# Transposed block inverse taken from a transpose of the updated one, in place of a third product per level

## The reference

```python
m = jnp.where(strict, jnp.einsum('bhnid,bhnjd->bhnij', kb, k) * decay, 0.0)
a_mat = m + jnp.eye(C, dtype=m.dtype)
rhs = jnp.concatenate([v * beta[..., None], kb * jnp.exp(gc)[..., None]], axis=-1)
uw = lax.linalg.triangular_solve(a_mat, rhs, left_side=True, lower=True, unit_diagonal=True)
```

## Time and profile before

| | us |
|---|---|
| median of three runs | 1123.85 |
| profiled execution, device time | 1124.4 |
| its span (first to last instruction) | 1122.6 |
| PE busy | 1055.5 (94%) |
| DVE busy | 707.6 (63%) |
| ACT busy | 582.1 (52%) |
| POOL busy | 116.7 (10%) |

### The profile page before, as it was taken

The page is one execution under the profiler, slowest core; times in us unless marked ns, Lnnn a source line. Parts: engine busy times, 40 slices in busy tenths (PEclk is TensorE's granted clock), DMA queues, the critical chain, the costliest instruction groups (busy, mean ns, idle before and its releaser), DMA issues. The chain is left out here.

```text
span 1122.6 us, 17149 instructions
## 1 busy us (share of the span) xinstructions
PE 1055.5 (94%) x7154; PEld 945.9 (84%) x7154; DVE 707.6 (63%) x1027; ACT 582.1 (52%) x869; POOL 116.7 (10%) x111
## 2 busy tenths in 40 slices
PE   2699988899999999999999999999999989999997
PEld 2599978888899788877988889988988969988996
DVE  5679775586685467577655656455446786555554
ACT  3355545643465455545567655444446886444443
POOL 1100016562040001122000010000000200000000
PEclk9999999999899999999999999999999999999999
DMA  9766433532368733223633336555553435555550
GB/s 325 231 187 187 149 115 112 188 114 82 84 187 255 260 122 113 75 76 113 205 133 113 112 123 216 188 187 184 189 183 121 150 126 185 193 186 188 181 181 37
DMA packets 120428, 178.42 MB, mean 159 GB/s; under 512 B 5188, under 2 KB 80098, under 8 KB 120352
## 3 DMA queue, kind: packets, MB, share of 16 engines
q1 hardware_dynamic: 118816, 172.40, 47.3%
q0 software_dynamic: 1120, 2.97, 0.9%
q10 hardware_dynamic: 416, 1.97, 0.5%
HBM read 176.27 MB, written 1.05 MB: 158 GB/s over the span
## 5 line engine op out<-in xcount | busy, mean ns | idle before, releaser
L1334 DVE TENSOR_TENSOR sb_w_lo<-sb_raw,sb_w_hi 128x2048 fp32r<-128x2048 f32 (+2 forms) x141 | 319.6, 2267 | 217.9 <-ACT sb_w_hi L705 217.6
L705 ACT ACTIVATE sb_w_hi<-sb_raw 128x2048 fp32r<-128x2048 f32 (+2 forms) x141 | 265.9, 1889 | 141.6 <-PE G L2135 112.2
L2133 PE MATMUL X<-sb_hT_hi,sb_w_hi 128*128 128x256 f32 x960 | 273.2, 285 | 4.0 <-DVE sb_hT_lo L1664 2.1
L2134 PE MATMUL X<-sb_hT_lo,sb_w_hi 128*128 128x256 f32 x960 | 271.1, 282 | 0.0
L2135 PE MATMUL X<-sb_hT_hi,sb_w_lo 128*128 128x256 f32 x960 | 271.0, 282 | 0.0
L2133 PEld LDWEIGHTS X<-sb_hT_hi,sb_w_hi 128*128 128x128 f32 x960 | 183.1, 191 | 6.5 <-issue 3.0
L2134 PEld LDWEIGHTS X<-sb_hT_lo,sb_w_hi 128*128 128x128 f32 x960 | 183.2, 191 | 0.6
L2135 PEld LDWEIGHTS X<-sb_hT_hi,sb_w_lo 128*128 128x128 f32 x960 | 183.2, 191 | 0.0
L2133 PE MATMUL G<-sb_w_hi,sb_uT_hi 128*128 128x512 f32 x304 | 121.5, 400 | 4.8 <-DVE sb_uT_lo L2073 4.8
L2135 PE MATMUL G<-sb_w_hi,sb_uT_lo 128*128 128x512 f32 x304 | 120.8, 397 | 0.0
L2134 PE MATMUL G<-sb_w_lo,sb_uT_hi 128*128 128x512 f32 x304 | 120.5, 397 | 0.0
(11 more groups left out here) (442 smaller groups left out, 1793.7 us busy)
## 6 DMA issues: line engine op xcount, KB each, us to landing
sb_raw<-in_mlp_w SPq DMA_DIRECT2D x64, 1024.0 KB, 5.3
sb_raw<-in_ada_w SPq DMA_DIRECT2D x24, 1024.0 KB, 5.1
sb_raw<-in_a_in_w SPq DMA_DIRECT2D x16, 1024.0 KB, 5.7
sb_raw<-in_b_in_w SPq DMA_DIRECT2D x16, 1024.0 KB, 5.5
sb_raw<-in_sb_w_qkv SPq DMA_DIRECT2D x12, 1024.0 KB, 5.2
sb_raw<-in_rg_w_in SPq DMA_DIRECT2D x8, 1024.0 KB, 5.4
sb_raw<-in_a_out_w SPq DMA_DIRECT2D x4, 1024.0 KB, 5.0
sb_raw<-in_b_out_w SPq DMA_DIRECT2D x4, 1024.0 KB, 5.0
```

The source lines that it names most:

```text
L705: nc.scalar.activation(w_hi[s][:, 0:nk * w], raw[b % RAW_SLOTS][:, 0:nk * w], ACT.Copy).then_inc(S["w_hi"], 1)
L1334: nc.vector.tensor_tensor(w_lo[s][:, 0:nk * w], raw[b % RAW_SLOTS][:, 0:nk * w], w_hi[s][:, 0:nk * w].bitcast(F32), ALU.subtract).then_inc ...
L2133: dt32(out, lh, rh, start=first, stop=False, skip_group_check=shared)
L2134: dt32(out, lh, rl, start=False, stop=False, skip_group_check=shared)
```

## The change

In levels 0 to 4 the third product (update of `ddT`) and its subtraction on DVE are gone. From level 1 on, after `dd` is updated and right behind the product L2466, PE transposes `dd` (four instructions) into the PSUM tile that took the third product, and ACT copies it to `ddT`. Level 5 keeps its only product (update of `ddT`) and gains transpose and copy too. On ACT the ada products and the two exponentials are dealt out between the copies.

```diff
@@ ACT
+                def inverse_copies(l):
+                    for m in range(MT):
+                        act.wait_ge(S["d1T"], turned(hg, l, m))
+                        nc.scalar.activation(ddT[m][:, :, :], quad((G[2], TB[1])[m]), ACT.Copy).then_inc(S["d1"], 1)
+                def decay(m):
+                    act.wait_ge(S["dec_arg"], 4 * hg + 2 + m + 1)
+                    nc.scalar.activation(at_[m][:, :, :], at_[m][:, :, :], ACT.Exp).then_inc(S["dec"], 1)
                 if hg == 1:
                     split_hi(first_mm["a_out"] + 1)
+                inverse_copies(1)
+                if hg == 1:
                     act.wait_ge(S["o1_sb"], 1)
...
-                ada_products(8 + 8 * hg)
-                if hg == 1:
-                    ada_products(17)
-                for m in range(MT):
-                    act.wait_ge(S["dec_arg"], 4 * hg + 2 + m + 1)
-                    nc.scalar.activation(at_[m][:, :, :], at_[m][:, :, :], ACT.Exp).then_inc(S["dec"], 1)
-                    if m == 0:
-                        ada_products(9 + 9 * hg)
-                for a in ((10, 11, 12, 13), (19,))[hg]:
-                    ada_products(a)
+                if hg == 0:
+                    ada_products(8)
+                for l in range(2, 6):
+                    inverse_copies(l)
+                    if l >= 3 and l < 5:
+                        decay(l - 3)
+                    ada_products(7 + l + 7 * hg)
+                if hg == 0:
+                    ada_products(13)
@@ DVE
                         if l < 5:
-                            nc.vector.tensor_tensor(dd[m][:, :, :], dd[m][:, :, :], quad((G[1], TB[0])[m]), ALU.subtract)
-                        nc.vector.tensor_tensor(ddT[m][:, :, :], ddT[m][:, :, :], quad((G[2], TB[1])[m]), ALU.subtract)\
-                            .then_inc(S["inv_d"], 1)
+                            nc.vector.tensor_tensor(dd[m][:, :, :], dd[m][:, :, :], quad((G[1], TB[0])[m]), ALU.subtract)\
+                                .then_inc(S["inv_d"], 1)
+                        else:
+                            dve.wait_ge(S["d1"], turned(hg, 5, m))
+                            nc.vector.tensor_tensor(ddT[m][:, :, :], ddT[m][:, :, :], quad((G[2], TB[1])[m]), ALU.subtract)\
+                                .then_inc(S["inv_d"], 1)
@@ PE
                         ins.then_inc(S["inv_g"], 1)
+                        if l >= 1:
+                            for h in range(4):
+                                ins = transpose(quad((G[2], TB[1])[m])[:, h, :], dd[m][:, h, :], ident)
+                            ins.then_inc(S["d1T"], 1)
...
                         pe.wait_ge(S["inv_gs"], j + 1)
+                        pe.wait_ge(S["d1"], turned(hg, l, m))
                         for h in range(4):
                             if l < 5:
-                                dt32(quad((G[1], TB[0])[m])[:, h, :], ddT[m][:, h, :], gs[m][:, h, :], start=True, stop=True)
-                            ins = dt32(quad((G[2], TB[1])[m])[:, h, :], gs[m][:, h, :], ddT[m][:, h, :], start=True, stop=True)
+                                ins = dt32(quad((G[1], TB[0])[m])[:, h, :], ddT[m][:, h, :], gs[m][:, h, :], start=True, stop=True)
+                            else:
+                                ins = dt32(quad((G[2], TB[1])[m])[:, h, :], gs[m][:, h, :], ddT[m][:, h, :], start=True, stop=True)
```

More of the change, by code:

```diff
@@ L514, in loaded, with turned @@
             return 16 * sum(loads(i) for i in range(b % RAW_SLOTS, b + 1, RAW_SLOTS))
+        def turned(hg, l, m):
+            return 12 * hg + 2 * l + m + 1
         def parts(call):
@@ L899, in _ @@
                 for m in range(MT):
-                    act.wait_ge(S["d1T"], 2 * hg + m + 1)
+                    act.wait_ge(S["d1T"], turned(hg, 0, m))
                     nc.scalar.activation(dd[m][:, :, :], quad((X[0], TB[1])[m]), ACT.Copy).then_inc(S["d1"], 1)
@@ L1587, in _ @@
                         if l == 0:
-                            dve.wait_ge(S["d1"], 2 * hg + m + 1)
+                            dve.wait_ge(S["d1"], turned(hg, 0, m))
                             dve.wait_ge(S["d1T_sb"], 2 * hg + m + 1)
@@ L2460, in _ @@
                         if l == 0:
-                            pe.wait_ge(S["d1"], 2 * hg + m + 1)
+                            pe.wait_ge(S["d1"], turned(hg, 0, m))
                             pe.wait_ge(S["mt"], 2 * hg + m + 1)
```

## The result

The changed kernel takes 1113.47 us (median of four runs, 1112.91 to 1113.65), beside 1123.96 us for the kernel before in the same measurement: a ratio of 0.9902, 95% interval 0.9888 to 0.9916, faster by 10.5 us. The forecast was 1113.4. That the two agree to a tenth is in part luck: the account further down has terms of 0.5 to 1.6 us that the sum did not have, and they cancel.

The account below looks back on a forecast made before the run. PE was taken to bound both head groups (busy 94% of the span). Gains of 7.2 us in group 0 and 3.45 in group 1 sum to 10.65, clock and late copies at 0, giving 1113.4 us; range 1110.0 to 1118.5.

Parts of the forecast that it names:

- PE work: Both groups, levels 0 to 5: 160 instructions (17.9 us) go, 80 transposes (8.8 us) come, net 9.1 us less.
- the saving of level 0: Level 0, both groups: 1.79 us less PE work per group, hidden because a DVE split stands ahead of the subtraction.
- The tail: End of group 0: block 13's load lands earlier, so `uu` is copied at 187.1 instead of 194.27, 7.2 us gained.
- The idle places before: PE idle in group 0 before: 0.45 us at level 1's start, 0.78 at the tail, 2.78 ahead of L2513.
- ACT in time: Group 0: ada blocks of 2.56 us fit between ACT's copies; tight, but no copy late.
- the rival of late copies: ACT copies late, about half a microsecond in ten levels: only 5.7 us gained, 1118 us; chance 0.20.
- The 0.3 us for the late exponential in level 4: Group 0, level 4: exponential behind ACT's second copy delays DVE's product and subtraction, adding 0.3 us.
- Group 1: Second head group: level 5 starts 4.2 us earlier, ada block 19 loses 0.75 us again, so `uu` gains 3.45 us.
- The clock, taken at 0: New clock falls behind level 0's idle, or old ones gone: -3.5 to +3.5 us, about 1.8 each, counted as 0.
- The range: Whole kernel: outer bounds 1110.0 to 1118.5 us; the narrow forecast, 1111 to 1116, had chance 0.62.
- Slower rival: Levels 1 to 5 at 1.2 GHz because transposes do not count as activity: 1126 us to +41 us; chance 0.05.
- the sixteen transposes of the earlier trace: At 309.28 to 310.95, 0.104 us each, clock full right behind them: cited as evidence that transposes do not lower the clock.

Follow-up runs that it names:

- transposes_twice: Changed kernel with each transpose of `dd` done twice into the same place, 80 transposes more: 1118.99 us, 0.9954 of the kernel before.
- ada_early: Kernel before, no transposes, with ACT doing group 0's ada blocks 9 and 10 ahead of the first exponential, 11 between the two: 1119.59 us, 0.9957.
- ada_late: Changed kernel with group 0's ada blocks 9 to 12 each put back one place on ACT: 1120.83 us, 0.9971 of the kernel before.
- fill_products: Changed kernel with 12 unread float32 products in PE's gap in level 0 of group 1: 1108.82 us, 0.9872 of the kernel before.
- long_transposes: Changed kernel with 400 unread transposes in PE's gap in level 0 of group 1: 1152.56 us, one run.
- split_after: Changed kernel with DVE's split in level 0 of group 1 moved behind the subtractions: 1109.30 us, 0.9871 of the kernel before.
- uu_first: Changed kernel with ada block 13 moved behind the copies of `uu` and `s1` in group 0: 1111.64 us, 0.9894 of the kernel before.
- both_filled: Changed kernel, group 1's level 0 split behind subtractions, group 0's ada block 13 behind `uu` and `s1`, 12 unread products before group 1's first transpose: 1108.72 us, 0.9863.

## Why the prediction was right

- **PE work.** 80 transposes at 0.11 us in place of 160 instructions at 0.1117: levels 1 to 5 start within 0.2 us of the forecast in group 0, the saving of level 0 stayed hidden as forecast, and `transposes_twice` shows that PE's work is on the path.
- **The tail.** `uu` moved 7.26 us (forecast 7.2), and from level 0 by 7.75 (44.76 to 37.01). Much of it hangs on ACT's order, which is the step least visible in the profile: without the transposes the order alone gave 3.5 us (`ada_early`), and with them and the old order `uu` came 4.55 us later (`ada_late`). The sum did not part the two. Two readings were off beside it. PE's product was done at 190.7, but PE worked on until 192.12, where the idle of 2.78 us begins; and by the forecast's own times (tail at 183.9 and 2.56 us of work behind it) the idle left would have been 1.3 us, not 1.5. Measured: 0.86.
- **The idle places before.** The list in the forecast leaves out 1.21 us ahead of L2484 in level 1 and 0.48 us in level 5. Its path has both all the same: level 1 was given 0.3 us of wait, and 0.20 was measured.
- **ACT in time.** All margins held, the rival of late copies did not come. The 0.3 us for the late exponential in level 4 was hardly there: level 5 started 0.05 us after PE was free. So ACT began block 12 about 0.3 us earlier than forecast, and blocks 12 and 13 took 4.9 us in place of 5.2; together these are about the 0.55 us by which group 0 beat the forecast.
- **Group 1.** From its level 0 to `uu` 39.88 us against 42.32 before, 2.44 gained where 3.45 were forecast. Level 1 lost 1.64 us (7.93 against 6.29 in `fill_products`) to the clock. Without that 4.1 would have been gained, 0.6 more than forecast: level 4 again had no wait for the exponential, and block 19 made `uu` only 0.2 us late, where the forecast let 0.75 be lost.
- **The clock, taken at 0.** This term was wrong in its parts and small in its sum: 1.64 us lost in level 1, 1.1 us won net between 252 and 310 us. A further 0.49 us was lost ahead of the change to the later load, which the forecast had no term for. So 7.75 + 4.1 of schedule, 0.1 lost between the groups, 0.5 lost to the load, 1.6 lost and 1.1 won by the clock make 10.7, the measured difference of the spans, beside a forecast of 10.65. The schedule alone was worth about 1.2 us more than forecast; that the total hit is the luck.
- **The range.** Its ends, 1110.0 and 1118.5, take the clock's and the copies' bounds one at a time; both at their worst would have been 3.5 + 5 us, near 1122. The measured 1113.47 lies in the narrow range, 1111 to 1116.
- **Slower rival.** The levels did not fall to half the clock as a whole, and `long_transposes` takes away the rival's ground. The one fall, in level 1 of group 1, goes with the idle ahead of it and not with the transposes, since it is gone in `fill_products` and `split_after`, which have the same transposes; at 1.64 us it was of the size named (1.8 us a time). The forecast's own ground against this rival was weaker than it reads: the sixteen transposes of the earlier trace rows ran at full pace from the first, so they did not bring the clock back, they only did not lose it in 1.7 us.

## What to carry to other kernels

Where PE fills a stage, a transpose of the updated tile (one instruction) with a copy on any engine that has room is cheaper than a second float32 product of the same size (two instructions and a subtraction). Follow each queue past the stage that the change is about: here about a third of the gain, 3.5 us, was a load that ended up earlier because its consumer's order had changed, and it could be had alone. And before claiming less than 2 us, compare the start times of the same instructions in the two traces, stage by stage: a load that landed 0.49 us later and a fall of the clock near 305 us were in this difference without belonging to the change. PE work that is taken out where another engine sets the end turns into idle, and the idle can cost the clock: in level 0 of group 1 it grew from 1.57 to 2.76 us, and 1.64 us were lost behind it.

## What the runs showed of the hardware that was not expected

Mean granted clocks differ from run to run of one kernel (0.981 to 0.995 for the kernel before). The time follows them only in part: the kernel with copies on DVE ran at 1109.18 us with 0.996 and at 1113.45 with 0.984, but the fastest run of `uu_first` (1110.51) had its lowest clock, 0.986.

One reason can be seen in the profiles. From 48 to 53 us the products of `hT_hi` and `hT_lo` start 0.21 us apart in the profiles of the kernel before and after alike, and 0.11 or 0.12 us apart from about 53 us on. So PE ran at half pace there in both, yet the window from 40 to 50 us has a granted clock of 1.00 before and of 0.50 after. Part of the difference between two mean clocks (0.990 and 0.984 in these profiles) is therefore in the record and not in the pace: the spacing of equal instructions is the surer measure.

Most falls lie behind waits of PE, but not each wait brings one: 2.78 us ahead of L2513 did not the earlier trace rows, 2.76 us in group 1 of the changed kernel did, and the 2.82 us ahead of the first transposes of group 1 did in the changed kernel and not in `fill_products`. And one fall has no idle time of PE in the 10 us ahead of it. In the kernel before, PE went from products of 512 columns through 32 products of one column, and was at half the clock behind them:

```profile
285.58 3.94 PE L2274 MATMUL X<-sb_consts,sb_ada_acc 128*128 128x1 f32 x32
```

```profile
290.00:295.00 5.00, 5.00 (x14) 3.83 (x13) 2.29 (x1) 0.00 (x0) 0.00 (x0) 0.50 0.20 39
```

The same products brought no fall in the profiles of `transposes_twice` and `both_filled`. What decides when the clock falls these runs do not show.
